# Context logits, softmax and top rounds ahead of the first expert's turned rows; the last expert's down products by chunks

## The reference, cut to what matters

```python
h2 = rms_norm(x, norm2_g) * (1.0 + scale2) + shift2
x = x + gate2 * expert_choice_moe(h2, w_router, w_gate, w_up, w_down)

def expert_choice_moe(h, w_router, w_gate, w_up, w_down):   # 16 experts
    aff = softmax(h @ w_router, axis=-1)                    # each token over the experts
    gates, idx = top_k(aff.T, cap)                          # each expert takes its best tokens:
                                                            # cap = 2 * N // 16, so 64 latents, 16 context tokens
    xe = h[idx]
    hid = silu(xe @ w_gate) * (xe @ w_up)                   # 1024 -> 2048
    ye = (hid @ w_down) * gates                             # 2048 -> 1024
    return zeros_like(h).at[idx].add(ye)
```

## Time and profile before

| what | value |
|---|---|
| median of 3 runs | 1715.78 us (1715.04 to 1717.36) |
| profiled execution, its own time | 1715.51 us |
| its span in the profile | 1713.7 us |
| TensorE busy | 1666.5 us, 97% of the span |
| VectorE, ScalarE, GpSimd busy | 565.4, 343.1 and 283.2 us |
| mean DMA rate over the span | 297 GB/s |

### The profile page before, as it was taken

The page is one execution under the profiler, slowest core; times in us unless marked ns, Lnnn a source line. Parts: engine busy times, 40 slices in busy tenths (PEclk is TensorE's granted clock), DMA queues, the critical chain, the costliest instruction groups (busy, mean ns, idle before and its releaser), DMA issues.

```text
span 1713.7 us, 32105 instructions
## 1 busy us (share of the span) xinstructions
PE 1666.5 (97%) x13964; PEld 863.8 (50%) x13964; DVE 565.4 (33%) x973; ACT 343.1 (20%) x702; POOL 283.2 (17%) x237
## 2 busy tenths in 40 slices
PE   6999999999999989899999999999999999999997
PEld 3767778778888778333333333333333333333332
DVE  3797527347677675211011011011011101101101
ACT  4533222246666733100000000000000000000000
POOL 1364403000010000101210220220220121121011
PEclk9999999999999999799999999999999999999998
DMA  9545644322132144899999999999999999999993
GB/s 338 174 155 200 229 158 136 103 89 88 41 97 86 46 168 190 336 420 412 410 420 412 411 417 414 411 411 420 411 412 420 412 411 420 412 411 418 413 413 126
DMA packets 122257, 508.56 MB, mean 297 GB/s; under 512 B 13084, under 2 KB 35060, under 8 KB 72968
## 3 DMA queue, kind: packets, MB, share of 16 engines
q1 hardware_dynamic: 111856, 484.80, 70.8%
q0 software_dynamic: 9520, 21.52, 4.5%
q10 hardware_dynamic: 744, 0.15, 0.0%
HBM read 487.02 MB, written 19.42 MB: 296 GB/s over the span
## 4 chain that ended last, share of the span: by engine, by line
PE 87%; DMA 5%; DVE 3%; POOL 2%; issue 1%; ACT 1%; SPq 0%; DVEq 0%; ACTq 0%; POOLq 0%
PE banks L2172 54%; PE banks L1785 7%; PE banks L1787 7%; PE banks L1786 7%; PE banks L2015 2%; PE banks L2002 2%; PE banks L1926 2%; DMA raw<-in_w_down_e 2%; DMA raw_w<-in_w_down_e 2%; PE banks L1810 1%; POOL qk_swp L1678 1%; POOL qk_swp L1673 1%; DMA raw<-in_w_ada 1%; PE banks L2112 1%; PE banks L1964 1%
## 5 line engine op out<-in xcount | busy, mean ns | idle before, releaser
L1785 PE MATMUL banks<-w_hi,h_hi 128*128 128x512 f32 x560 | 225.7, 403 | 3.8 <-DVE w_lo L1105 3.0
L1634 DVE TENSOR_TENSOR hid<-banks,sg 128x512 f32<-128x512 f32 x48 | 31.1, 673 | 598.7 <-PE banks L2172 598.7
L1787 PE MATMUL banks<-w_lo,h_hi 128*128 128x512 f32 x560 | 219.5, 392 | 0.0
L1786 PE MATMUL banks<-w_hi,h_lo 128*128 128x512 f32 x560 | 218.9, 391 | 0.0
L1750 POOL DMA_INDIRECT out<-yeg_c,idx_c x64 | 83.6, 1306 | 812.4 <-DVE yeg_c L1619 797.8
L1084 ACT ACTIVATE sg<-banks 128x512 f32<-128x512 f32 x48 | 25.2, 598 | 905.9 <-PE banks L2172 905.9
L2172 PE MATMUL banks<-raw_k,xe 128*32 128x512 f32 x1536 | 167.8, 592 | 0.0
L2172 PE MATMUL banks<-raw,xe 128*32 128x512 f32 x1152 | 129.7, 602 | 0.7 <-issue 0.7
L2172 PE MATMUL banks<-raw_x,xe 128*32 128x512 f32 x1152 | 126.6, 592 | 0.0
L1785 PEld LDWEIGHTS banks<-w_hi,h_hi 128*128 128x128 f32 x560 | 105.6, 189 | 36.3 <-issue 11.8
L1787 PEld LDWEIGHTS banks<-w_lo,h_hi 128*128 128x128 f32 x560 | 105.5, 188 | 23.2
(11 more groups left out here) (261 smaller groups left out, 2049.4 us busy)
## 6 DMA issues: line engine op xcount, KB each, us to landing
raw_k<-in_w_up_e SPq DMA_DIRECT2D x32, 1024.0 KB, 27.4
raw_k<-in_w_gate_e SPq DMA_DIRECT2D x32, 1024.0 KB, 25.8
raw_k<-in_w_down_e SPq DMA_DIRECT2D x32, 1024.0 KB, 26.3
raw<-in_w_in SPq DMA_DIRECT2D x26, 1024.0 KB, 5.9
raw<-in_w_gate_e SPq DMA_DIRECT2D x24, 1024.0 KB, 25.7
raw_x<-in_w_up_e SPq DMA_DIRECT2D x24, 1024.0 KB, 24.1
raw<-in_w_down_e SPq DMA_DIRECT2D x24, 1024.0 KB, 27.5
raw_x<-in_w_gate_e SPq DMA_DIRECT2D x24, 1024.0 KB, 26.7
```

The costliest lines, as they stand in the source:

```text
L1634: nc.vector.tensor_tensor(hid[:, part, :].rearrange("p (f a j) -> p f a j", j=STRIP, a=2), in_turn(bank(3 + part)), in_turn(sg[:, part, :] ...
L1785: nc.tensor.matmul(ps, hi, wh, start=first, stop=False)
L1786: nc.tensor.matmul(ps, lo, wh, start=False, stop=False)
L1787: return nc.tensor.matmul(ps, hi, wl, start=False, stop=last)
```

## The change

Five edits, all of order:

1. In `context_behind()` the logits, exponential, division, affinities' transposition and the context's two rounds (`L`, `P`, `U`, `A`, `K`, `K`) stand ahead of the first expert's turned rows (`E`, 0); the two index steps `F` and `G` stand behind them.
2. TensorE now leaves `F` and `G` out of the list's order, in place of `A` and `F`, and does both behind the first chunk of the first gate.
3. GpSimd no longer waits for both index steps ahead of the context's first gather; it waits for `F` only, and for `G` ahead of the second expert's gathers.
4. Twelve filler transposes are put ahead of the context's first transposes (`X`, NL, 0), in a bank that nobody reads then.
5. The last expert's down products are ordered by chunks (`last_down`, `LAST_AHEAD = 2`): for chunk i the context's products, then the latents' of chunk i - 2, and the latents' of the last two chunks at the end. The signals `context_done` and `latent_done` follow the last product of each sum.

```diff
--- before.py
+++ after.py
@@ -247,6 +247,7 @@
 QUARTER = D // 4
 PARTS = (2, 0, 1)
 AHEAD = 6
+LAST_AHEAD = 2
 EXPERT_SLOT = [2, 0, 1, NRAWE + 8] + [NRAWE + i for i in range(4, 8)] + list(range(NRAW, NRAWE)) + [NRAWE + i for i in (2, 3, 0, 1, 9)]
 NEX = len(EXPERT_SLOT)
 
@@ -270,8 +271,8 @@
 def context_behind():
 
     steps = [("W", NL, 0), ("W", NL, 1), ("D", 0)] + [("K", i) for i in range(CAP_L // 8)] + [("J", 0), ("J", 1)]
-    steps += [("V", 0), ("V", 1), ("N", NL, 0), ("X", NL, 0), ("N", NL, 1), ("X", NL, 1), ("R", NL), ("S", NL), ("E", 0), ("L", NL), ("P", NL), ("G", 0)]
-    return steps + [("U", 1), ("A", 1), ("K", CAP_L // 8), ("K", CAP_L // 8 + 1), ("F", 0), ("E", 1)]
+    steps += [("V", 0), ("V", 1), ("N", NL, 0), ("X", NL, 0), ("N", NL, 1), ("X", NL, 1), ("R", NL), ("S", NL), ("L", NL), ("P", NL)]
+    return steps + [("U", 1), ("A", 1), ("K", CAP_L // 8), ("K", CAP_L // 8 + 1), ("E", 0), ("F", 0), ("G", 0), ("E", 1)]
 
 
 STEPS = [("M", 0), ("T", 0), ("O", 0), ("Q", 0), ("B", 0), ("Q", 1), ("M", 1), ("W", 0, 0), ("T", 1), ("H", 0), ("M", 2), ("T", 2), ("M", 3), ("W", 1, 0), ("T", 3), ("M", 4),
@@ -279,7 +280,7 @@
 BEFORE = {("T", 2): ("W", 1, 0), ("T", 3): ("W", 2, 0), ("T", 4): ("W", 3, 0), ("A", 0): ("W", NL, 0)}
 BEFORE.update({("X", ORDER[p - 1], 1): ("W", ORDER[p], 1) for p in range(1, NL)})
 SQUARES = [step[1:] for step in STEPS if step[0] == "N"]
-MEANWHILE = {"J": 16, "E": 8}
+MEANWHILE = {"J": 16, "X": 12, "E": 8}
 AHEAD_OF_A = 1
 EARLY_TILES = 1
 ROUTER_UNIT = 5
@@ -1590,13 +1591,13 @@
                         last = nc.vector.tensor_scalar(idx_l[rows, :], older[rows, :], 2.0, float(i), ALU.mult, ALU.add)
                     last.then_inc(p2_emptied, 1)
                 elif what == "F":
+                    dve.wait_ge(quarter_in, 16)
                     ps = piece2(("F", 0, 0))
                     nc.vector.tensor_scalar(idx_g[2][:, :], ps[:, 0:E], 4.0, quarter[:, 0:1], ALU.mult, ALU.add).then_inc(idxg_ready, 1)
                     for i in range(4):
                         nc.vector.tensor_scalar(idx_c[i][:, :], ps[0:CAP_C, 0:E], 4.0, float(i), ALU.mult, ALU.add)
                     nc.vector.tensor_copy(gate_c4[:, :], ps[:, E:2 * E]).then_inc(p2_emptied, 1)
                 elif what == "G":
-                    dve.wait_ge(quarter_in, 16)
                     ps = piece2(("G", 0, 0))
                     nc.vector.tensor_scalar(idx_g[0][:, :], ps[:, 0:E], 4.0, quarter[:, 0:1], ALU.mult, ALU.add).then_inc(idxg_ready, 1)
                     nc.vector.tensor_scalar(idx_g[1][:, :], ps[:, E:2 * E], 4.0, quarter[:, 0:1], ALU.mult, ALU.add).then_inc(p2_emptied, 1)
@@ -1767,9 +1768,9 @@
             pool.wait_ge(idxg_ready, 1)
             pool.wait_ge(xn_out[PLACE[NL] % 2], 16 * (NL // 2 + 1))
             pool.wait_ge(x2c_out, 16)
-            pool.wait_ge(idxg_ready, 2)
             wait_emptied(pool, ("F", 0, 0))
             gather(0, range(PARTS_X - 1, PARTS_X))
+            wait_emptied(pool, ("G", 0, 0))
             for e in range(E):
                 if e + 1 < E:
                     gather(e + 1, range(PARTS_X))
@@ -2093,6 +2094,8 @@
                     output_part(step, AHEAD_OF_A if step == BEFORE["A", 0] else CK if step in BEFORE.values() else 0, KT)
                 elif what == "X":
                     half = half[0]
+                    if (t, half) == (NL, 0):
+                        meanwhile(MEANWHILE["X"], ROW_BANK[0])
                     if half == 0:
                         pe.wait_ge(x2_first, t + 1)
                     else:
@@ -2159,11 +2162,11 @@
                         last = nc.tensor.matmul(ps[:, g * E:(g + 1) * E], spread[:, g, :], older[:, :], start=True, stop=True)
                     finished((what, t, 0), last)
 
-            late = [("A", 1), ("F", 0)]
+            late = [("F", 0), ("G", 0)]
             for step in STEPS:
                 if step not in late:
                     stage_step(step)
-            for step in (("X", NL, 1), ("W", NL, 1), ("G", 0, 0)):
+            for step in (("X", NL, 1), ("W", NL, 1), ("A", 1, 0)):
                 wait_emptied(pe, step)
 
             def in_strips(out, left, right, first, last):
@@ -2199,15 +2202,34 @@
                     if i in (0, 4):
                         pe.wait_ge(xe_ready, i // 4 + 1)
                     if i == 1:
-                        stage_step(("A", 1))
-                    if i == 4:
                         stage_step(("F", 0))
+                        stage_step(("G", 0))
                     pe.wait_ge(*expert_loaded(0, 0, i))
                     for part in range(2):
                         hidden_part(0, part, i, expert_buffer(0, i))
                 pe.wait_ge(xec_ready, 1)
                 for i in range(KT):
                     hidden_part(0, 2, i, expert_buffer(0, i)).then_inc(chunk_read, 1)
+
+            def last_down(e, odd):
+
+                def down_chunk(down, i):
+                    for f in (2 * i, 2 * i + 1):
+                        last = down(f, down_rows(odd, f))
+                    return last
+
+                for i in range(EC - ES):
+                    pe.wait_ge(*expert_loaded(e, odd, ES + i))
+                    last = down_chunk(down_context, i)
+                    if i == EC - ES - 1:
+                        last.then_inc(context_done, 1)
+                    if i == LAST_AHEAD:
+                        pe.wait_ge(ht_ready, e * 2 + 2)
+                    if i >= LAST_AHEAD:
+                        last = down_chunk(down_latent, i - LAST_AHEAD)
+                for i in range(EC - ES - LAST_AHEAD, EC - ES):
+                    last = down_chunk(down_latent, i)
+                last.then_inc(latent_done, 1)
 
             def expert(e, odd, first, last_e):
                 if first:
@@ -2225,24 +2247,22 @@
                 if not first:
                     pe.wait_ge(yeg_ready, e * 2)
                 pe.wait_ge(ht_ready, e * 2 + 1)
-                for f in range(FE // P if last_e else AHEAD):
+                if last_e:
+                    last_down(e, odd)
+                    return
+                for f in range(AHEAD):
                     if f % 2 == 0:
                         pe.wait_ge(*expert_loaded(e, odd, ES + f // 2))
-                    last = down_context(f, down_rows(odd, f))
-                if last_e:
-                    last.then_inc(context_done, 1)
+                    down_context(f, down_rows(odd, f))
                 pe.wait_ge(ht_ready, e * 2 + 2)
                 for f in range(FE // P):
-                    if not last_e and f >= AHEAD and f % 2 == 0:
+                    if f >= AHEAD and f % 2 == 0:
                         pe.wait_ge(*expert_loaded(e, odd, ES + f // 2))
                     last = down_latent(f, down_rows(odd, f))
-                    if not last_e:
-                        if f >= AHEAD:
-                            last = down_context(f, down_rows(odd, f))
-                        if f % 2 == 1:
-                            last.then_inc(chunk_read, 1)
-                if last_e:
-                    last.then_inc(latent_done, 1)
+                    if f >= AHEAD:
+                        last = down_context(f, down_rows(odd, f))
+                    if f % 2 == 1:
+                        last.then_inc(chunk_read, 1)
 
             expert(0, 0, True, False)
             with nc.Fori(1, E - 2, 2, engines=[pe.engine], hint_back_edge=True) as e:
```

## The result

The changed kernel takes 1705.56 us (median of 4 runs, 1704.01 to 1707.26), the kernel before 1715.64 beside it (4 runs, 1715.04 to 1717.36): 10.1 less by the medians. The ratio is 0.9938, with a 95% interval of 0.9923 to 0.9953. The forecast was 1706.5, with a range of 1702.0 to 1709.8.

The account below looks back on a forecast made before the run. Bound by one long weight stream opened by X, then by GpSimd's stores at the end. Span 1713.7 less 2.0 (front) and 7.3 (tail) is 1704.4; plus 1.8 and 0.27 gives 1706.5, range 1702.0 to 1709.8.

Parts of the forecast that it names:

- X: Start of the first gate's context products on TensorE; forecast to move from 719.24 to 717.2, the loop behind unchanged.
- T: Reference event at the front that the edits don't touch: transposes of the context's second half, 688.99 before, 690.02 after.
- The front: Work ahead of the first gate's context products: their start comes 2.0 earlier, 719.24 to 717.2.
- The gather's path: Context rows' gather on GpSimd: issued at 707.5, not 713.88, after the rows' store lands; 8.2 to land, at 715.7.
- TensorE's stretch: Latents' products of the eight first-gate chunks: 17.25 plus 0.6 from a start at 699.3, ending at 717.2.
- The start: TensorE's first wide products begin at 699.3, not 701.99; early bound 698.2, late bound near 699.6.
- the clock's return: TensorE's full clock in the first gate comes back some 5.5 after the start; 3 sooner or later changes 1.5.
- the prediction's own signs of being wrong: X moving less than TensorE's start, last chunk not 973.04 from X, or GpSimd idling ahead of the last store.
- The tail: GpSimd's five adding stores in a row set the end; latents' store issued at 1701.16, not 1708.48: 7.3 gained.
- the latents' 8.1: Last expert's latents' products end at 1698.9, 8.1 earlier; said not to be the gain.
- Rival 2: Front opens fully: clock holds, gather finds the queue drained, X at 712.9, 6.3 gained, 1702.2; chance 0.12.
- Rival 4: Slower: TensorE stays at half clock through the tail, latents done 10.5 later, 1724.3; chance 0.04.

Follow-up runs that it names:

- the front alone: Changed kernel with the old order of the last expert's down products, against the kernel before: 1713.82 against 1716.51, ratio 0.9984.
- the two single edits: Changed kernel with GpSimd's wait for the residual's store moved behind the first gather, or the context rows' store on ScalarE's queue: ratios 0.9941 and 0.9936 to the kernel before.
- The tail alone: Kernel before with only the last expert's down products ordered by chunks: 1709.30 against 1716.51, ratio 0.9958.
- both gather edits: Changed kernel with the context rows' store on ScalarE's queue and GpSimd's residual-store wait moved: 1701.68 with fillers, 1704.97 without; ratios 0.9920 and 0.9937 to the kernel before.

## Why the prediction was right

**What bounds.** That the loop only moves with X was the base of the sum. Over the eight profiles with `LAST_AHEAD` = 2, X - T goes from 23.89 to 29.65, and the last store stays at 981.5 to 982.4 behind X; with the old tail it is at 989.2 in both profiles, and the last chunk 972.96 behind X in the front alone. Right.

**The front, 2.0 forecast.** 2.6 by X - T in the changed kernel's profile, 2.7 (1.2 to 4.3) by the time of the front alone. The gather's path held: issue forecast 18.5 behind T, measured 19.1; landing price 8.2 taken, measured 7.1; X forecast 28.2, measured 27.66. The two errors go against each other, which is luck: alone they would have put X 0.6 later or 1.1 sooner. The forecast named the wait, the rows' store behind the chunk loads, and it was that. The residual's store, which the code also has GpSimd wait for, is not in the prediction; it ends 1.3 sooner in the changed kernel, and the two single edits show that it would have held the gather almost as long.

**TensorE's stretch was the wrong step.** I had it tie with the gather at 717.2, 28.2 behind T. It ended 23.95 behind T in one execution and 25.25 in another (717.96 - 1.89 - 690.82). Two terms were mis-sized. The start: I put it nearer to the bound at half clock (10.3 behind T); the fillers held the clock at 1.00 into the logits, and it was 9.1, the early bound's 9.2. And the clock's return: I kept the 5.5 behind the start; it came just ahead of the start in the first execution (0.81 in 698 to 699) and 3.6 behind it in the second (at 703). One of the prediction's own signs of being wrong came true by this: X moved less (2.6) than TensorE's start (13.0 to 9.1 behind T, 3.9). It didn't show in the sum only because the gather's path, a separate one, had come out at the same instant; that the error fell on the side that the gather hides is luck. Without fillers the start is 10.35 behind T, the value that I had taken, and there TensorE's stretch does set X.

**The tail, 7.3 forecast.** 6.8 by the last store behind X (7.1 to 7.7 in the other kernels with that tail), 7.2 by the time of the tail alone. Front and tail together are 9.4 in the profiles, against 9.3 forecast, so a front that was 0.6 too small and a tail that was 0.5 too large nearly made each other up. The forecast said that the latents' 8.1 would not be the gain, and GpSimd's row would; LAST_AHEAD = 1 shows that. The 0.5 that is missing in the changed kernel is the context's sum: its fourth store goes 980.84 behind X, 1.06 later than before (979.78), where 0.55 was forecast. It fits TensorE's wait ahead of X, after which it came back at half clock and the context products of the first chunks took longer (4.24 for three chunks, 2.76 before); no other profile with this tail has that stretch, but none was made to show it.

**Rivals.** Rival 2 (X at 712.9, 6.3 gained) came true in another kernel by its size, not by its mechanism: with both gather edits X is 23.89 behind T, 6.4 less than before, but there the gather went some 5.4 sooner and still took 6.9 to land, with the stream full. What kept it out here was the wait for the stores and, as was put against it, the loads that fill the queue. Rival 4 didn't happen with two chunks of trail and showed in part with four: there the clock fell behind waits on loads, which the forecast had said would be gone with two. The Trainium skill's rule on groups shorter than their waits ("TensorE: Matmul & The Clock Gate", "HAM oscillation — how this bites in real kernels") agrees with that row, 1.93 against 1.07, and with the changed kernel's pairs, which have no waits and stay at full clock.

## What to carry to other kernels

Where a saturated stream follows a start-up, look for the one event that opens it, and price an edit by how far it moves that event; everything behind it is a shift. Name all the waits in front of that event with the time that each ends: if two end nearly together, half an edit is worth next to nothing, and a small store that queues behind megabytes of loads is such a wait. At the end, don't price an edit by the engine that it relieves but by the row of issues that comes next.

## What the hardware showed that I had not expected

The clock came back at different places in executions of one program: just ahead of the first wide products and 3.6 behind their start in two profiles of the changed kernel; why, the runs don't show. Reckoning an edit's worth from one profile's clock is uncertain by that.

Twelve transposes of the identity, in TensorE's wait ahead of the context's transposes, kept the clock at 1.00 through 688 to 691 where it is at half without them; the logits behind them took 1.9 to 2.6 in eight profiles, in place of 3.4 in the two without fillers and of 3.6 in the kernel before.

The rows' store of 512 KB landed 14.0 to 14.8 behind its issue on SyncE's queue, behind chunk loads (nine profiles), and 9.1 to 9.3 on ScalarE's queue at the same place (three), while the residual's store, left on SyncE's, went from 16.9 to 17.3 up to 18.0 to 18.2.
